# The front stage makes its own constants, stores the bias spread in four quarters, reads packed weights; attention loads by 512 tokens

## The reference, cut to what matters

```
h = rms_norm(x, norm_gain);  proj = h @ w_in            # split into c_q, c_kv, k_pe, q_b, k_b, v_b, q_i, k_i, w_i, gates
q_a = rms_norm(c_q, mla_q_norm)   @ mla_w_uq            # 8 heads of 96
kv  = rms_norm(c_kv, mla_kv_norm) @ mla_w_ukv           # 8 heads: 64 of k, 64 of v
q_a, k_a = rms_norm per head, rope on the last 32;  q_b, k_b = rms_norm per head, rope on the first 16
o_a = causal softmax(q_a k_a^T) v_a                      # "mla": 8 heads
o_b = softmax over the 256 keys picked by the index scores (q_b k_b^T) v_b   # "dsa": 8 heads, 2 kv heads
...
bias = t5_table[bucket(distance)]                        # used much later, by the windowed attention
```

## Time and profile before

| | us |
|---|---|
| median of 3 runs (lowest, highest) | 3619.01 (3615.78, 3619.95) |
| the profiled execution, its own time | 3615.94 |
| its span in the profile | 3614.1 |
| PE busy | 3165.4 (88%) |
| DVE busy | 2055.4 (57%) |
| ACT busy | 1825.8 (51%) |
| POOL busy | 815.7 (23%) |
| front stage, first x load issued to last store issued | 6.4 to 494.9 |
| mla stage, first load issued | 501.1 |
| dsa stage, first load issued | 1725.1 |

### The profile page before, as it was taken

The page is one execution under the profiler, slowest core; times in us unless marked ns, Lnnn a source line. Parts: engine busy times, 40 slices in busy tenths (PEclk is TensorE's granted clock), DMA queues, the critical chain, the costliest instruction groups (busy, mean ns, idle before and its releaser), DMA issues. The chain is left out here.

```text
span 3614.1 us, 50019 instructions
## 1 busy us (share of the span) xinstructions
PE 3165.4 (88%) x16696; PEld 2632.8 (73%) x16696; DVE 2055.4 (57%) x5101; ACT 1825.8 (51%) x3632; POOL 815.7 (23%) x1091
## 2 busy tenths in 40 slices
PE   1999959999949899998499996987969999969998
PEld 1788848888837777777367774766858888859997
DVE  2577648888825556565499886432136666642112
ACT  2566536767726566665477774002236666643221
POOL 1544421111033221111111101011214444311110
PEclk8999969999979999999699997998989999979999
DMA  6466672243172222221621104655352222144332
GB/s 137 143 207 204 194 175 55 66 95 86 25 242 87 72 71 73 74 66 66 127 48 40 31 19 140 190 164 186 133 170 68 71 69 67 45 119 156 117 117 70
DMA packets 344638, 386.92 MB, mean 107 GB/s; under 512 B 68768, under 2 KB 269264, under 8 KB 339648
## 3 DMA queue, kind: packets, MB, share of 16 engines
q1 hardware_dynamic: 330544, 335.17, 33.2%
q0 software_dynamic: 13840, 48.58, 4.2%
HBM read 224.48 MB, written 159.19 MB: 106 GB/s over the span
## 5 line engine op out<-in xcount | busy, mean ns | idle before, releaser
L76 PE MATMUL i_p_g<-i_hT_lo,i_wh 128*128 128x512 f32 x768 | 310.5, 404 | 6.0 <-issue 5.1
L78 PE MATMUL i_p_g<-i_hT_hi,i_wh 128*128 128x512 f32 x768 | 306.6, 399 | 0.0
L77 PE MATMUL i_p_g<-i_hT_hi,i_wl 128*128 128x512 f32 x768 | 305.8, 398 | 0.0
L1509 DVE SCALAR_TENSOR_TENSOR i_score<-i_relu,i_w,i_score 128x1024 f32<-128x1024 f32 (+7 forms) x154 | 156.1, 1024 | 191.1 <-ACT i_relu L1383 188.8
L1394 ACT ACTIVATE i_above<-i_score,i_less 128x384 bf16<-128x384 f32 (+13 forms) x140 | 182.9, 1307 | 88.9 <-POOL i_less L1460 68.2
L1028 DVE TENSOR_TENSOR mla_tl<-mla_p_t,mla_th 128x512 fp32r<-128x512 f32 (+1 forms) x320 | 186.1, 606 | 45.0 <-ACT mla_th L1071 43.1
L1071 ACT ACTIVATE mla_th<-mla_p_t 128x512 fp32r<-128x512 f32 (+1 forms) x320 | 164.0, 529 | 88.2 <-PE mla_p_t L968 85.6
L998 DVE CUSTOM_DVE_ANT_0 dsa_probs<-dsa_p_s,dsa_mask 128x512 f32<-128x512 f32 (+3 forms) x320 | 184.6, 605 | 42.2 <-PE dsa_p_s L1638 40.5
L1383 ACT ACTIVATE i_relu<-i_p_s 128x1024 f32<-128x1024 f32 (+7 forms) x176 | 141.6, 809 | 125.9 <-DVE i_score L1506 83.7
L1028 DVE TENSOR_TENSOR dsa_tl<-dsa_p_t,dsa_th 128x512 fp32r<-128x512 f32 x272 | 179.9, 686 | 39.2 <-ACT dsa_th L1071 34.0
L1637 PE MATMUL dsa_p_s<-dsa_k_hi,dsa_q 128*128 128x512 f32 (+3 forms) x320 | 132.3, 415 | 70.5 <-DMA dsa_k_lo<-scratch_kbT 45.5
(11 more groups left out here) (342 smaller groups left out, 9470.7 us busy)
## 6 DMA issues: line engine op xcount, KB each, us to landing
scratch_gates<-i_ob SPq DMA_DIRECT2D x96, 256.0 KB, 2.4
m_m<-scratch_gates SPq DMA_DIRECT2D x64, 256.0 KB, 4.0
f_hs<-scratch_h2T SPq DMA_DIRECT2D x16, 1024.0 KB, 9.8
scratch_qkT<-b_th SPq DMA_DIRECT2D x64, 192.0 KB, 2.6
scratch_qkT<-b_tl SPq DMA_DIRECT2D x64, 192.0 KB, 3.1
i_ws<-in_w_in SPq DMA_DIRECT2D x24, 512.0 KB, 4.6
b_xt<-in_x SPq DMA_DIRECT2D x16, 512.0 KB, 4.9
scratch_h<-b_xh POOLq DMA_DIRECT2D x16, 512.0 KB, 3.0
```

Of the source, the lines that this page charges most:

```text
L76: pe.matmul(out, l[0], r[1], start=start, stop=False)
L77: pe.matmul(out, l[1], r[0], start=False, stop=False)
L78: return pe.matmul(out, l[0], r[0], start=False, stop=stop)
L1509: nc.vector.scalar_tensor_tensor(out=acc, in0=r, scalar=w[:, t, h:h + 1], in1=acc, op0=ALU.mult, op1=ALU.add).then_inc(summed, 1)
```

## The change

The stage of constants is gone. `ident` is written by POOL at the head of the front stage, the product for `t_row` is made inside it on the bank `p_u[2]`, and the store of the spread is cut into four quarters of 4 rows each, issued by SP at slot 8 of tiles 3, 5, 7 and 9. The weights of the projections come packed by the host (layout alone) as 12 arrays of 128 rows by 4 KB; gains and positions are packed too; there are 5 slots instead of 3 (two more on `b_sq`), and the angles move from `b_sq` to `b_th`, so POOL no longer waits for the constants before the angles. v is kept and stored interleaved: high and low of a head side by side, 4 KB and 1 KB per token. mla loads head 0 in four groups of 512 tokens; dsa loads keys and values in four groups of 512 tokens, and a tile waits for its own group.

The diff, cut to its core:

```diff
-        raw = [qk[:].rearrange("p a n -> p (a n)")[:, x * D:(x + 1) * D] for x in range(3)]
+        raw = [qk[:].rearrange("p a n -> p (a n)")[:, x * D:(x + 1) * D] for x in range(3)] + [
+            sq[:, x * D:(x + 1) * D] for x in range(2)]
+        slots = len(raw)
+        bias.start(sem, c, p_u[0:WH, 2, 0:3 * P])
...
             for n in range(n_w):
-                x, k = divmod(2 * n, KD)
-                if n >= 3:
-                    sp.wait_ge(w_lo, 2 * (n - 3) + 2)
-                dst = raw[n % 3].rearrange("p (k n) -> p k n", n=GT)
-                for c0, w, at in PARTS[x][0]:
-                    sp.dma_start(dst[:, :, at:at + w], view[:, k:k + 2, c0:c0 + w]).then_inc(w_in[n], 16)
+                if n >= slots:
+                    sp.wait_ge(w_lo, 2 * (n - slots) + 2)
+                sp.dma_start(raw[n % slots], a["w_front_p"][n]).then_inc(w_in[n], 16)
...
+            bias.load(sp)
             for n in range(n_slots + 1):
...
+                if s == 8 and i in (3, 5, 7, 9):
+                    bias.store(sp, (i - 3) // 2)
...
+            bias.vector(dve)
             dve.wait_ge(w_lo, 3 * KD + 3)
...
-            pool.wait_ge(const_in, 16 * 6)
+            g.memset(ident[:], 0.0)
+            pool.drain()
+            g.affine_select(out=ident[:], in_=ident[:], compare_op=ALU.not_equal, fill=1.0, base=0,
+                            pattern=[[-1, P]], channel_multiplier=1).then_inc(ident_made, 1)
             angle_tables()
...
+                if n == 4:
+                    bias.tensor(pe)
...
     def load(self, sp, n):
+        if h == 0:
+            at, blocks = slice(g * GT, (g + 1) * GT), slice(4 * g, 4 * g + 4)
+            done = self.first_in[g]
+        elif g == 0:
+            at, blocks, done = slice(0, T), slice(0, NT), self.in_[p]
...
+        for group in range(NG) if t == 0 else ():
+            self.load_keys(sp, group)
...
+    def store(self, sp, piece):
+        h = slice(piece * WH // self.pieces, (piece + 1) * WH // self.pieces)
         sp.wait_ge(self.filled, 2)
-        sp.dma_start(self.spread, self.row[:].unsqueeze(1).broadcast_to([WH, P, 3 * P]))\
+        sp.dma_start(self.spread[h], self.row[h].unsqueeze(1).broadcast_to([WH // self.pieces, P, 3 * P]))\
             .then_inc(self.stored, 16)
```

More of the change, by code:

```diff
@@ L217, in raw_of @@
         def raw_of(x, k):
-            return raw[(x * KD + k) // 2 % 3][:, k % 2 * GT:k % 2 * GT + PARTS[x][1]]
+            return raw[(x * KD + k) // 2 % slots][:, k % 2 * GT:k % 2 * GT + PARTS[x][1]]
         def rotate(ops, eng, x, table, t, tmp, done):
@@ L241, in store_values @@
                 sp.wait_ge(v_lo, 3 * t + 3)
-                for half, src in ((0, vh), (1, vl)):
-                    sp.dma_start(va[half, rows(t), :], src[:, 0:512].bitcast(F32)).then_inc(v_stored, 16)
-                    sp.dma_start(vb[half, rows(t), :], src[:, 512:640].bitcast(F32)).then_inc(v_stored, 16)
+                for dst, h0, h1 in ((va, 0, H), (vb, H, H + KV)):
+                    sp.dma_start(dst[rows(t), :], vv[:, h0:h1].rearrange("p h x d -> p (h x d)").bitcast(F32))\
+                        .then_inc(v_stored, 16)
             def store_turned(t, b):
@@ L2716, in _ @@
                 finish(t)
-def stage_constants(nc, sem, ident, bias):
-    made = sem("ident_made")
-    with (nc.psum_tensor("t_ps", [WH, 3 * P], F32) as ps, nc.sbuf_tensor("t_hot", [32, 3 * P], F32) as hot,
-          nc.sbuf_tensor("t_tab", [32, WH], F32) as tab):
-        bias.start(sem, hot, tab, ps)
-        with nc.Block() as block:
-            @block.sync
-            def _(sp):
-                bias.sync(sp)
-            @block.tensor
-            def _(pe):
-                bias.tensor(pe)
-            @block.vector
-            def _(dve):
-                bias.vector(dve)
-            @block.gpsimd
-            def _(pool):
-                nc.gpsimd.memset(ident[:], 0.0).then_inc(made, 1)
-                pool.wait_ge(made, 1)
-                nc.gpsimd.affine_select(out=ident[:], in_=ident[:], compare_op=ALU.not_equal, fill=1.0,
-                                        base=0, pattern=[[-1, P]], channel_multiplier=1).then_inc(made, 1)
 def program(nc, a, out):
@@ L2762, in program @@
         rs = c.enter_context(nc.sbuf_tensor("rs_2", [P, NT], F32))
-        with ExitStack() as c1:
-            bias = BiasJob(a["one_hot"], a["t5_table_2"], spread)
-            bias.setup(nc, c1)
-            stage_constants(nc, sem, ident, bias)
-            sem.end_stage()
-            stage_front(nc, sem, ident, a, h_dram, qkT, qbT, kbT, qiT, kiT, va, vb, wi, bias)
-            sem.end_stage()
+        bias = BiasJob(nc, a["one_hot"], a["t5_table_2"], spread)
+        stage_front(nc, sem, ident, a, h_dram, qkT, qbT, kbT, qiT, kiT, va, vb, wi, bias)
+        sem.end_stage()
         stage_attention(nc, sem, "mla", ident, Mla(qkT, va, oaT))
@@ L2787, in program, with front_layouts @@
         sem.end_stage()
+def front_layouts(given):
+    by_part = lambda x, n: np.ascontiguousarray(x.reshape(n, P).T)
+    w = given["w_in"][0]
+    packed = np.zeros((3, KD, P, GT), w.dtype)
+    for part, (columns, _) in enumerate(PARTS):
+        for c0, n, at in columns:
+            packed[part, :, :, at:at + n] = w[:, c0:c0 + n].reshape(KD, P, n)
+    packed = packed.reshape(3 * KD // 2, 2, P, GT).transpose(0, 2, 1, 3).reshape(3 * KD // 2, P, 2 * GT)
+    return {"w_front_p": np.ascontiguousarray(packed), "norm_gain_p": by_part(given["norm_gain"], KD),
+            "c_gain_p": by_part(np.concatenate([given["mla_q_norm"][0], given["mla_kv_norm"][0]]), 3),
+            "positions_p": by_part(given["positions"], NT)}
 _INS = ["x", "positions", "norm_gain", "w_in", "b_merge", "mla_q_norm", "mla_w_uq", "mla_kv_norm",
```

164 lines of the change are left out of this document (82 added, 82 removed).

## The result

The changed kernel took 3656.7 us (median of 4 runs, 3651.3 to 3662.8) against 3619.5 for the kernel before beside it (4 runs, 3615.8 to 3620.7): 1.0105 times as long, 95% interval 1.0088 to 1.0123. It is slower by 37 us. The profiled execution took 3656.5 us with a span of 3654.6, so the spans differ by 40.5.

A forecast was written before the change was run, and what follows sets the result against it. PE, busy 88% of the span, was taken as the bound, so only its idle stretches count. From 3619.0 us, 49 + 8 + 2.5 = 59.5 gained makes 3559.5; 89 for four quarters makes 3648, range 3595 to 3690.

The forecast's parts named there:

- Start: Front stage's beginning: x and weights land earlier, the wait for angles and a low-clock stretch go; 49 us gained.
- The angles: POOL's angles in the setup: they start well under 20 us, take 29, and ACT's wait for them is gone.
- mla: Start of the mla stage: the first group is 1 MB instead of 3 MB; 8 us gained (6 to 9).
- dsa: Start of the dsa stage: less to load before the first matmul; 2.5 us gained (-2 to 13).
- the second start: PE's start on dsa's tile 1: stays near 1763.16, as its q is issued behind all keys and values.
- A quarter takes 34 us: Spread store in the front stage: a quarter reading 4 partitions takes 34 us, as long as the whole store.
- 6.1 GB/s for each partition: Rate of the spread's store: set by the partitions it touches, so a quarter of 4 partitions moves at 24.5 GB/s.
- The stall: Front stage behind each quarter: a later store lands late and ACT, then PE, wait; 22.3 us each, 89 for four.
- ScalarE's arrears: Behind each quarter: ACT redoes its delayed work, x turns first, before PE's next bank is free; about 1 us.
- PE restarts at the low clock: Behind each quarter's hole in PE: running at the low clock costs 1.7 to 3.3 us.
- The rival of short quarters: Spread's quarters take 8.5 us each and land before anyone needs the ring: 3560 us, faster by 1.6%; chance 0.14.
- what the rest of the change is worth: Start, mla and dsa without the spread: 59.5 us gained, which makes 3559.5 us.

The follow-up runs named there:

- e7: e4 with the first loads of both attention stages whole, over all tokens, instead of in groups of 512: 3573.3 us.
- e10: e9 with a semaphore of their own for each group's values, so the first score matmul waits for four loads instead of five: 3537.7 us.
- e6: e4 with q and mask of dsa's tile 1 loaded behind key group 0 instead of behind key groups 0 to 3: 3548.9 us.
- e9: e6 with dsa's key groups 1, 2 and 3 issued behind the q and mask of tiles 2, 3 and 4: 3545.5 us.
- e3: The changed kernel with each quarter issued as four DMAs of one row, one partition each, spread over all engines: 3646.2 us.
- e12: The changed kernel with quarter p storing rows p, p+4, p+8 and p+12 instead of four adjacent rows: 3559.7 us.
- e5: The changed kernel with the four quarters issued by ScalarE at the same slots instead of by SyncE: 3652.1 us.
- e2: The changed kernel with each quarter reading all 16 rows and writing a quarter of the copies, same bytes and places: 3559.0 us.
- e4: The changed kernel with each row held eight times, in 128 partitions; a quarter reads all 128 and writes four copies from each: 3553.5 us.
- e11: The changed kernel with the 16 rows of the spread in partitions 96 to 111 instead of 0 to 15: 3656.9 us.
- e8: e4 with three raw weight slots instead of five in the front's setup: 3565.1 us.

## Why the prediction was right

The forecast was 3648 us, slower; measured 3656.7. Step by step:

- *Start, 49 us.* It gave 53.3. Two us of the miss are x: I had it at ScalarE at 6.3 and VectorE's first low half at 15.8, the profile has 4.24 and 13.84. One more is in the weights: I had the last chunk at ScalarE from 31.5, the profile has it at 28.38, 3.1 earlier with the two of x. The tail behind it was 10.9 us where I had 11.4 and 0.7 for VectorE's new work. The angles are off the path, as foreseen: POOL ends them at 42.74 + 0.93 = 43.7, and ScalarE comes to the sine at 48.35 without a wait. They took POOL 36 us (from 7.4 on) where I had 29, since one of its operations took 7.40 us where its like take 1.3 (last section).
- *mla, 8 us.* 6.0 us in the two profiles, 5.7 to 8.1 over the eleven other kernels with these loads (all but e7). TensorE began 8.2 us after the first load, not 6.6. The term was right but for the fifth load: I counted its bytes and not that it lands last; e10 takes that wait away and finds 6.7.
- *dsa, 2.5 us.* 3.1 in the profiles; 499.7, 498.4, 502.9, 500.7, 501.1, 500.0, 501.6, 500.3 and 496.8 us in the nine kernels with these loads against 502.8. The reason is shown by e6 and e9: the second start is bound by q's place in the order. The first start came 13.2 us earlier, near the 14 that I gave it (2.5 MB less at 212 GB/s would have made 11.8).
- *A quarter takes 34 us.* Right in size: 26 to 33 us by the rates in the windows, and ScalarE goes on 37.2 us after the issue of the first, where I had 35.5; no landing of a quarter stands in the trace. The ground I gave is half wrong. I had read "6.1 GB/s for each partition" out of 98 GB/s for 16. Single partitions one behind another move 27 to 29 GB/s (e3), four adjacent ones 24 to 30, and behind four that stand four apart ScalarE goes on after 14.7 us instead of 37.2 (e12). What fits all of these is that the time goes by how many groups of neighbours a transfer reads; how wide such a group is, no run measures. With adjacent rows both readings give the same number, and that is why the forecast came out: for rows four apart it would have given the same 34 us and been wrong (e12). That the size came out was luck. The two rules of the Trainium skill that I weighed part here: "SBUF — State Buffer", section "Door 1: The DMA port swizzle", has four neighbours share one port, and e3 and e12 agree; "DMA: Bandwidth & Descriptors", section "Rules for kernel authors", has four outer rows confine the DMA to four engines, which the share of 0.24 bears out, but e12 has four outer rows too and loses next to nothing.
- *The stall, 22.3 us for each.* 24.3 (97.3 for four): 8.3 us more than foreseen, which the 4.3 that the start gave more offset by half. The waits sum to 99.6 on ScalarE. PE's holes are 22.3 us on average where I had 20.3 (19.3 and 1 for ScalarE's arrears). That PE restarts at the low clock held: 0.54 in 159.4 to 163, and about 5 us of it behind each of the other three quarters, so that half speed costs an estimate of 1.6 to 2.6 us, within my 1.7 to 3.3 but for the first. The reason given for the wait was wrong in part. I let the store stand behind the quarter in SyncE's queue, since x had landed behind the spread; e5 gives the quarter another queue and 90.4 us of waits remain.
- *What I did not have.* The index stage, 6.0 us longer. Its instructions and loads are unchanged, and in the thirteen kernels behind the kernel before it took from 713.8 to 722.3 us, with the kernel before's 714.4 inside. So the 6.0 us are within a scatter of about 8 us in this stage and not shown to be an effect of the change. There is one profile for each kernel; that single executions scatter is likely, as the four of the changed kernel lie 11 us apart, but what makes this stage scatter is open.

Taken together: 53.3 + 6.0 + 3.1 + 0.4 - 97.3 - 6.0 = -40.5 us. The median moved by 37.3 us where I had 29. The rival of short quarters would have given 3560, and that is where e2, e4 and e12 stand, whose quarters are short: what the rest of the change is worth was right (59.5 us foreseen, 61.6 found in e2 against the 3620.6 of the kernel before beside it).

## What to carry to other kernels

The time of a transfer out of few partitions of SBUF goes by where they stand. Cut it in pieces so that each piece still reads all of the groups of neighbours (by copies, or every fourth row), or each piece takes nearly as long as the whole and stalls the stage again. Another queue was no cover against such a transfer (e5). A load that is brought forward to end a wait moves the wait to the next load behind it: order the whole chain by when each piece is needed. Where one wait covers several loads, ask which of them lands last, not only how many bytes they are.

## What the runs showed of the hardware

- DMAs of one source partition each, one behind another, over all engines: 27 to 29 GB/s at a DMA share of 0.87. Four adjacent ones on a quarter of the engines: 24 to 30 at 0.24. Sixteen: 98 to 100 at 0.91. All 128: 313. A high share of busy DMA does not show that the engines are the limit.
- A slow transfer from four partitions holds up stores that are issued to another queue (e5, until 37.6 us after its issue) or that read other partitions (e11, 101.9 us of waits in four), nearly for its whole length. Both at once was not tried.
- The same index stage took 713.8 to 722.3 us in fourteen profiled executions. A difference of a few us between two profiles has to be looked for in the stage where the edit is.
- One POOL operation in the angles took 7.40 us in the changed kernel, the next of the same shape 1.30. It is no single case: one took 7.4 to 7.8 us in each of the twelve kernels with five slots. It ends 1.0 us after VectorE's unbroken run of twelve subtractions (13.84 to 20.68). With three slots (e8, second view) that run ends at 17.49 and the POOL operation, now of 3.90 us, again 1.0 us later. So it waits out VectorE's run; which resource the two share, and why later subtractions (from 22.35) don't hold POOL so, is open.

```profile
14.30 7.40 POOL L618 TENSOR_TENSOR b_th<-b_cos,b_th 128x448 f32<-128x448 f32 x1
...
19.39 1.29 DVE L561 TENSOR_TENSOR b_wl<-b_qk,b_wh 128x512 fp32r<-128x512 f32 x2
...
23.34 1.30 POOL L618 TENSOR_TENSOR b_th<-b_cos,b_th 128x448 f32<-128x448 f32 x1
```

```profile
14.15 3.34 DVE L562 TENSOR_TENSOR b_wl<-b_qk,b_wh 128x456 fp32r<-128x456 f32 x6
...
14.61 3.90 POOL L619 TENSOR_TENSOR b_th<-b_cos,b_th 128x448 f32<-128x448 f32 x1
```
